# Two slabs of a state-space projection formed by seven block products, with the stage's parameters loaded a stage earlier

## The reference, cut to what matters

```
zxbcdt = x @ w_in                      # (256,1024) @ (1024,6208)
z, xbc, dt = split(zxbcdt, [2048, 6144])
xbc = silu(conv5(xbc, conv_w) + conv_b)    # depthwise over the tokens
xs, bm, cm = split(xbc, [2048, 3072])
dt = softplus(dt + dt_bias)
y = scan forwards (xs, dt_f, -exp(a_log[0]), bm, cm) + scan backwards + xs * d_skip
y = rms_norm_by_group(y * silu(z)) * norm_w
return y @ w_out
```

## Time and profile before

| | us |
|---|---|
| median of 3 runs | 2305.78 |
| lowest and highest | 2304.95 and 2306.76 |
| the profiled execution: its time | 2306.97 |
| its span, first to last instruction | 2305.1 |

### The profile page before, as it was taken

One profiled execution on the slowest core, in us unless ns is written; L12 is line 12 of the kernel. 1 busy time (PEld: TensorE's weight loads), 2 busy tenths in 40 slices (PEclk: granted clock), 3 DMA queues, 4 the chain that ended last, 5 costly groups with the idle time before them and its releaser, 6 DMA issues.

```text
span 2305.1 us, 25572 instructions
## 1 busy us (share of the span) xinstructions
PE 2269.1 (98%) x10790; PEld 1371.1 (59%) x10790; DVE 979.0 (42%) x1950; ACT 443.7 (19%) x1011; POOL 73.8 (3%) x130
## 2 busy tenths in 40 slices
PE   9999999999999999999999999999999999999998
PEld 6568547886487459997434433335999643333342
DVE  3567646667576557653211111125774311111122
ACT  3410003258110011220211211101132121111111
POOL 2000000000000000000000000000000000000000
PEclk9999999999999999999999999999999999999999
DMA  7279625354698415246999999995426599999997
GB/s 292 113 306 401 257 78 204 147 183 173 243 407 327 178 59 203 97 176 262 382 429 427 427 427 428 427 418 193 164 96 247 223 409 427 427 429 427 427 428 285
DMA packets 59168, 671.64 MB, mean 291 GB/s; under 512 B 7505, under 2 KB 7793, under 8 KB 18721
## 3 DMA queue, kind: packets, MB, share of 16 engines
q1 hardware_dynamic: 51888, 649.45, 69.1%
q0 software_dynamic: 7152, 20.43, 2.6%
HBM read 666.59 MB, written 3.26 MB: 291 GB/s over the span
## 4 chain that ended last, share of the span: by engine, by line
PE 87%; DMA 10%; DVE 3%; issue 0%; ACT 0%; SPq 0%; POOL 0%; DVEq 0%; POOLq 0%; ACTq 0%
PE ps L101 84%; DMA ring<-in_exp_w 8%; DVE arena L114 1%; PE ps L349 1%; DVE arena L117 1%; DMA arena<-ssm_rows 1%; PE ps L2753 1%; DMA ring<-in_ada_w 0%; PE ps L638 0%; DMA ring<-in_attn_w_in 0%; PE ps L1915 0%; DVE X L117 0%; PE ps L1234 0%; ACT arena L106 0%; DVE arena L110 0%
## 5 line engine op out<-in xcount | busy, mean ns | idle before, releaser
L101 PE MATMUL ps<-arena 128*64 128x512 f32 (+8 forms) x4036 | 954.6, 465 | 16.2 <-DMA arena<-in_exp_w 5.9
L101 PEld LDWEIGHTS ps<-arena 128*128 128x128 f32 (+2 forms) x4036 | 462.4, 167 | 464.5 <-issue 434.6
L101 PE MATMUL ps<-ring,arena 128*64 128x512 f32 (+2 forms) x1720 | 460.7, 584 | 3.2 <-DMA ring<-in_exp_w 3.2
L101 PE MATMUL ps<-XTGB,ring 128*128 128x256 f32 (+1 forms) x2160 | 423.5, 353 | 0.0
L101 PEld LDWEIGHTS ps<-XTGB,ring 128*128 128x128 f32 x2160 | 367.4, 191 | 52.5 <-issue 11.2
L101 PEld LDWEIGHTS ps<-ring,arena 128*64 128x64 f32 (+1 forms) x1720 | 174.9, 151 | 259.5 <-issue 253.9
L122 DVE COPY arena<-ps 128x512 f32<-128x512 f32 (+5 forms) x133 | 63.3, 496 | 417.4 <-PE ps L101 298.6
L121 ACT COPY arena<-ps 128x512 f32<-128x512 f32 (+3 forms) x179 | 81.5, 474 | 676.2 <-PE ps L2753 283.7
L101 PE MATMUL ps<-XTGB,arena 128*64 128x512 f32 (+2 forms) x736 | 200.7, 428 | 0.0
L105 ACT ACTIVATE arena<-ps 128x512 f32<-128x512 f32 (+2 forms) x95 | 51.2, 545 | 679.4 <-PE ps L101 674.6
L101 PE MATMUL ps<-ring,XTGB 128*128 128x512 f32 (+3 forms) x484 | 168.5, 503 | 2.9 <-DMA ring<-in_attn_w_in 2.7
(11 more groups left out here) (151 smaller groups left out, 949.8 us busy)
## 6 DMA issues: line engine op xcount, KB each, us to landing
arena<-in_exp_w SPq DMA_DIRECT2D x90, 2048.0 KB, 26.7
ring<-in_exp_w SPq DMA_DIRECT2D x68, 2048.0 KB, 27.9
ring<-in_mlp_w SPq DMA_DIRECT2D x25, 2048.0 KB, 8.8
ring<-in_ada_w SPq DMA_DIRECT2D x20, 2048.0 KB, 9.6
XTGB<-in_exp_w SPq DMA_DIRECT2D x18, 2048.0 KB, 32.3
ring<-in_ssm_w_in SPq DMA_DIRECT2D x12, 2048.0 KB, 7.6
ring<-in_w_in SPq DMA_DIRECT2D x12, 2048.0 KB, 7.8
ring<-in_gate_w SPq DMA_DIRECT2D x12, 2048.0 KB, 7.5
```

Source lines behind the costliest of these rows:

```text
L101: return self.e.matmul(o, lhsT=lhsT, rhs=rhs, start=start, stop=stop, skip_group_check=True)
```

## The change

Slabs 5 and 6 are formed by seven products of blocks in place of eight. The slab is cut into halves of its input channels and of its columns, `XT` into halves of its input channels and of the tokens; with the blocks X1, X2 (channels) and W the four blocks, the products are of single blocks (1 and 2), or of sums of blocks (3 to 7). VectorE forms the sums: four of `XT`'s blocks once (`sw_x_sums`), four of the weights' blocks for each slab (`sw_sums`, three of them, one in place in the slab, and `sw_last_sum`). The sums for slab 5 and three of those for slab 6 stand at the end of `mlp0_dve`, ahead of the row pass; slab 6's last one stands behind the first convolution. A product is 2 column blocks x 4 chunks = 8 matmuls with 128 moving columns; the seven go into four banks a slab (`SW_GROUPS`). ScalarE copies product 1 straight into an input buffer of the convolution, VectorE adds the others there (`sw_results`), and the copy of the whole bank falls away for these slabs. There are four input buffers in place of two, so eight memsets of the edges in place of four, and VectorE waits for them at its start as well. The four parameter loads move from `ssm_pool` to `mlp0_pool`.

```diff
--- before.py
+++ after.py
@@ -1106,6 +1106,10 @@
             pool.stage("mlp0")
             pool.wait_ge(at("XT", 1, 1))
             ada_b_pool(pool, 0, ab0)
+            pool.landed(pool.e.dma_start(prm, d["ssm_conv"].rearrange("p (a b) -> p a b", a=32)), "ssmp", "ssmp")
+            pool.landed(pool.e.dma_start(dd, d["ssm_dn"]), "ssmp", "ssmp")
+            pool.landed(pool.e.dma_start(dtb, bcast(d["ssm_dt_bias"][0:1, :])), "ssmp", "ssmp")
+            pool.landed(pool.e.dma_start(ang, bcast(d["ssm_A_log"][0:1, :])), "ssmp", "ssmp")
             keep_mod(pool, 0)
             for t in range(2):
                 rstd(pool, lrs[:, t:t + 1], at("var", 2, t), ("rstd", 2, t))
@@ -1128,6 +1132,10 @@
             for t in range(2):
                 blocks_out(v, 0, 2, t, sU0)
                 norm_turned(v, 2, t)
+            sw_x_sums(v)
+            sw_sums(v, 5)
+            sw_last_sum(v, 5)
+            sw_sums(v, 6)
             norm_rows_all(v, 2, at("gb", "ln2"))
 
 
@@ -1145,7 +1153,7 @@
         dtt = arena.get(2, 64)
         aa = arena.get(2, 64)
         s_pos = arena.pos
-        s_u = [arena.get(2, 260) for _ in range(2)]
+        s_u = [arena.get(2, 260) for _ in range(4)]
         s_v = [arena.get(2, T) for _ in range(2)]
         s_tok = arena.get(2, 512)
         CONV = [2, 3, 0, 1] + list(range(4, 16))
@@ -1163,6 +1171,93 @@
         tri = C["tri"]
         LE, GE, LEO, OGE = tri[:, 0:P], tri[:, 384:512], tri[:, 0:T], tri[:, T:512]
         drow = nc.dram_tensor("ssm_rows", (16, 1024), F32).ap()
+        room = arena.pos
+        arena.pos = zT.shape[1] * T + xcT.shape[1] * T
+        swX = [arena.get(4, P) for _ in range(4)]
+        swS = [[arena.get(4, T) for _ in range(2)] for _ in range(2)]
+        swS4 = arena.get(4, T)
+        arena.pos = room
+        SW_GROUPS = ((1, 6), (5, 7), (3, 4), (2,))
+        def conv_in(n):
+            return s_u[n % 2 + (2 if n in (4, 5) else 0)]
+        def sw_x_sums(v):
+            x1, x2, x3, x4 = swX
+            v.wait_ge(at("XT", 2, 0), at("XT", 2, 1))
+            k = v.then_inc(v.tt(x1, XT[:, 0:4, P:T], XT[:, 0:4, 0:P], ALU.subtract), "swX")
+            v.then_inc(v.tt(x3, XT[:, 4:8, P:T], XT[:, 0:4, P:T], ALU.subtract), "swX")
+            v.wait_ge(k)
+            k = v.then_inc(v.tt(x2, XT[:, 4:8, P:T], x1, ALU.subtract), "swX")
+            v.wait_ge(k)
+            v.then_inc(v.tt(x4, XT[:, 4:8, 0:P], x2, ALU.subtract), "swX")
+        def sw_sums(v, s):
+            w = weights(("sw", s))
+            s1, s2 = swS[s % 2]
+            v.wait_ge(at("w", ("sw", s)))
+            k = v.then_inc(v.tt(s1, w[:, 0:4, T:2 * T], w[:, 4:8, T:2 * T], ALU.add), ("swS", s, 5))
+            v.wait_ge(k)
+            k = v.then_inc(v.tt(s2, s1, w[:, 0:4, 0:T], ALU.subtract), ("swS", s, 6))
+            v.then_inc(v.tt(w[:, 0:4, T:2 * T], w[:, 0:4, 0:T], w[:, 0:4, T:2 * T], ALU.subtract), ("swS", s, 7))
+        def sw_last_sum(v, s):
+            s1, s2 = swS[s % 2]
+            v.wait_ge(at("swS", s, 6), at("swp", s - 1, 2) if s == 6 else None)
+            v.then_inc(v.tt(swS4, weights(("sw", s))[:, 4:8, 0:T], s2, ALU.subtract), ("swS", s, 3))
+        def sw_products(pe, s):
+            w = weights(("sw", s))
+            s1, s2 = swS[s % 2]
+            x1, x2, x3, x4 = swX
+            pairs = {1: (XT[:, 0:4, 0:P], w[:, 0:4, 0:T]), 2: (XT[:, 4:8, 0:P], w[:, 4:8, 0:T]), 3: (XT[:, 4:8, P:T], swS4),
+                     4: (x4, w[:, 4:8, T:2 * T]), 5: (x1, s1), 6: (x2, s2), 7: (x3, w[:, 0:4, T:2 * T])}
+            pe.wait_ge(at("w", ("sw", s)), at("swX"))
+            for r, group in enumerate(SW_GROUPS):
+                ps = bank(pe, "swp", s, r)
+                for n, p in enumerate(group):
+                    x, y = pairs[p]
+                    if p in (3, 5, 6, 7):
+                        pe.wait_ge(at("swS", s, p))
+                    for f in range(2):
+                        for c in range(4):
+                            ins = pe.mm(ps[:, n * T + f * P:n * T + (f + 1) * P], y[:, c, f * P:(f + 1) * P], x[:, c, :],
+                                        c == 0, c == 3)
+                pe.then_inc(ins, ("swp", s, r), *([("free", ("sw", s))] if r == 3 else []))
+        def sw_product(s, r, n):
+            return ps_of("swp", s, r)[:, n * T:(n + 1) * T].rearrange("p (f t) -> p f t", f=2)
+        def sw_parts(s):
+            n = 0 if s == 5 else 4
+            return [conv_in(n + k)[:, :, o:o + P] for k in range(2) for o in (2, 2 + P)]
+        def sw_results(v, s, r):
+            c11, c12, c21, c22 = sw_parts(s)
+            def plus(o, q, n, x, *done):
+                return v.then_inc(v.tt(o, sw_product(s, q, n), x, ALU.add), ("read", "swp", s, q), *done)
+            v.wait_ge(at("swp", s, r))
+            if r == 0:
+                v.wait_ge(at("swP1", s))
+                plus(c12, 0, 1, c11, ("swU2", s))
+            elif r == 1:
+                v.wait_ge(at("swU2", s))
+                e = plus(c21, 1, 1, c12)
+                plus(c12, 1, 0, c12, ("swU4", s))
+                v.wait_ge(e)
+                plus(c22, 1, 0, c21, ("conv in", s, 1), ("swU3", s))
+            elif r == 2:
+                v.wait_ge(at("swU3", s), at("swU4", s))
+                plus(c12, 2, 0, c12, ("conv in", s, 0))
+                plus(c21, 2, 1, c21, ("conv in", s, 1))
+            else:
+                plus(c11, 3, 0, c11, ("conv in", s, 0))
         SP = 16
 
         def ssm_sp(sp):
@@ -1176,10 +1271,6 @@
         def ssm_pool(pool):
             pool.stage("ssm")
             pool.wait_ge(at("XT", 2, 1))
-            pool.landed(pool.e.dma_start(prm, d["ssm_conv"].rearrange("p (a b) -> p a b", a=32)), "ssmp", "ssmp")
-            pool.landed(pool.e.dma_start(dd, d["ssm_dn"]), "ssmp", "ssmp")
-            pool.landed(pool.e.dma_start(dtb, bcast(d["ssm_dt_bias"][0:1, :])), "ssmp", "ssmp")
-            pool.landed(pool.e.dma_start(ang, bcast(d["ssm_A_log"][0:1, :])), "ssmp", "ssmp")
             for u in s_u:
                 pool.then_inc(pool.e.memset(u[:, :, 0:2], 0.0), "u0")
             for u in s_u:
@@ -1258,7 +1349,10 @@
                     turn_rows(pe, 2, 1, X, at("x", 2, 1))
                 gemm_t1(pe, ("sdt",), "sdt", 64, t)
             for s in range(5, 12):
-                gemm_f(pe, ("sw", s), ("sw", s), 4)
+                if s < 7:
+                    sw_products(pe, s)
+                else:
+                    gemm_f(pe, ("sw", s), ("sw", s), 4)
                 if s == 5:
                     for fp in range(2):
                         ps = bank(pe, "sw", 4, fp)
@@ -1333,6 +1427,12 @@
                 act.wait_ge(at("st", t))
                 act.then_inc(act.cp(s_tok[:, t, :], ps_of("st", t)), "s tok", ("read", "st", t))
 
+            def first_product(s):
+                act.wait_ge(at("swp", s, 0))
+                act.then_inc(act.cp(sw_parts(s)[0], sw_product(s, 0, 0)), ("swP1", s), ("read", "swp", s, 0))
+            first_product(5)
             def conv_out(n):
                 i = CONV[n]
                 act.wait_ge(at("conv", i))
@@ -1340,12 +1440,17 @@
 
             for n, i in enumerate(CONV):
                 s, fp, f0 = 4 + i // 2, i % 2, 2 * i
-                u, v_ = s_u[n % 2], s_v[n % 2]
-                act.wait_ge(at("sw", s, fp))
+                u, v_ = conv_in(n), s_v[n % 2]
+                if n == 3:
+                    first_product(6)
                 if n >= 2:
                     act.wait_ge(at("conv", CONV[n - 2]))
-                k = act.then_inc(act.cp(u[:, :, 2:258], two(ps_of("sw", s, fp))), ("read", "sw", s, fp))
-                act.wait_ge(k)
+                if s in (5, 6):
+                    act.wait_ge(at("conv in", s, fp), at("xc", CONV[n - 2]) if n >= 2 else None)
+                else:
+                    act.wait_ge(at("sw", s, fp))
+                    k = act.then_inc(act.cp(u[:, :, 2:258], two(ps_of("sw", s, fp))), ("read", "sw", s, fp))
+                    act.wait_ge(k)
                 for q in range(2):
                     act.then_inc(act.act(v_[:, q, :], u[:, q, 0:T], ACT.Identity, scale=prm[:, f0 + q, 0:1],
                                          bias=prm[:, f0 + q, 5:6]), ("conv0", i, q))
@@ -1412,10 +1517,10 @@
 
         def ssm_dve(v):
             v.stage("ssm")
-            v.wait_ge(at("XT", 2, 1), at("ssmp"))
+            v.wait_ge(at("XT", 2, 1), at("ssmp"), at("u0"))
 
             def conv(n, i):
-                u, v_ = s_u[n % 2], s_v[n % 2]
+                u, v_ = conv_in(n), s_v[n % 2]
                 for q in range(2):
                     f = 2 * i + q
                     v.wait_ge(at("conv0", i, q))
@@ -1440,8 +1545,17 @@
             k = v.then_inc(v.ts(aa, dtt, -1.0, None, ALU.mult))
             v.wait_ge(k)
             v.then_inc(v.tt(aa, aa, dtt, ALU.min), "dt min")
+            for r in range(4):
+                sw_results(v, 5, r)
             for n, i in enumerate(CONV):
                 conv(n, i)
+                if n == 0:
```

(6 more changed lines are left out.)

## The result

The changed kernel takes 2311.89 us (median of 8 runs, 2308.77 to 2315.44), the kernel before 2305.57 (8 runs beside them): ratio 1.0029, 95% interval 1.0019 to 1.0039. It is slower by 6.3 us, outside the range of 2302.5 to 2308.5; the forecast was no change.

What follows compares the result with a forecast made beforehand. TensorE, busy 98% of the span, was taken as the bound; slab 5's +0.66 us, including a 2.0 us stall, and slab 6's saving of 1.33 summed to -0.7 us: 2305.1 us forecast, range 2302.5 to 2308.5.

Steps and rivals of the forecast that it cites:

- The products: TensorE, slabs 5 and 6: 112 records of 0.1115 us make 12.49 us a slab, saving 1.33 each, 2.66 together.
- (2): Slabs 5 and 6: products show no gain at 0.127 us a record; +1.8 us, 2307.6; chance 0.14 together with (4).
- (3): Slabs 5 and 6: weight loads do not hide behind 128 columns; +15 us, 2321; chance 0.04.
- the estimate of 324 ns a matmul: TensorE's block products: four passes of about 81 ns per f32 matmul, 18.1 us a slab, some 8.7 us lost.
- The sums, the row pass, the memsets, the bank: Stage start: VectorE's sums delay row pass, memsets and ScalarE's copy, so TensorE stalls 2.0 us at slab 5's third bank.
- (1): Slab 5: no wait at the third bank; -2.66 us, 2303.1; chance 0.16.
- the sum: Whole change: slab 5 takes 0.66 us more, slab 6 saves 1.33, together -0.7 us.
- (4): Slab 6's last sum misses its 1.6 us margin; with 2 us beyond, +1.3, 2307.1; chance 0.14 together with (2).
- The cover of the moved loads: Parameter loads left in place would land some 11 us after first issue, TensorE standing still that long; the move covers this.
- moves with TensorE alone: Behind slab 6: VectorE, some 6 us later, catches up by slab 10, so only TensorE's change shifts the scan's start.
- what was not seen: Anywhere in the program: effects outside the named cases, chance 0.04, half to each side.

Runs made afterwards that it cites:

- early edges: Changed kernel with the eight edge memsets moved from the state-space stage to right behind the moved parameter loads: 2308.97 us, ratio 1.0016.
- padded changed kernel: Changed kernel with 16 matmuls added to the first expert stage's general path, which is jumped over and never runs: 2307.65 us, ratio 1.0011.
- the padding: 16 matmuls added to the never-run path; on the changed kernel with the edge memsets also moved early: 2303.33 us, ratio 0.9992.
- 44 matmuls: Kernel before with 44 matmuls added to the general path that is jumped over and never runs: 2305.09 us in a single execution.

## Why the prediction was wrong

**The products.** Right: 32 records from 362.73 to 366.30 are 0.1116 us each, 0.1115 was taken; without the wait two slabs save 45.58 - 42.96 = 2.62 us, 2.66 was the sum. Rivals (2) and (3) are out. With them goes, for these f32 products, the estimate of 324 ns a matmul that the prediction made by the pairing rule of the Trainium skill's "TensorE: Matmul & The Clock Gate" ("Back-to-back issue gap"): the trace has 223.

**The sums, the row pass, the memsets, the bank.** Right in each link: the row pass ends 362.91 + 4.87 = 367.8 us, ScalarE starts at 369.7 (370.4 and 372.2 in the prediction, both less the 2.9 us of the span's start: 367.5 and 369.3), and TensorE waits 2.12 us, where 2.0 was said. Rival (1) is out in the changed kernel; the early edges show that it takes only the memsets' place to make it true. The stage gains 0.25 us in the profiled execution, 0.7 was the sum: TensorE resumes at 370.37, 0.3 us later than said (372.95 less 2.89). VectorE adds seven results a slab, not the eight that the prediction counted (12 sums and 14 additions are the 26 instructions that it has more); no wait of TensorE depended on it. No wait shows inside slab 6 or behind slab 8, so rival (4) is out. The cover of the moved loads was sized too high: with the loads in their old place the last one landed 6.3 us behind the first one's issue (369.27 to 375.59), not 11, and TensorE stood still for 8.0 us.

**What the wait costs.** Mis-sized in one of the two executions profiled that have it. In the padded changed kernel the same wait of 2.13 us is followed by a product at half pace, 3.48 us instead of 1.89:

```profile
368.54 1.95 PE L101 MATMUL ps<-arena,ring 128*128 128x128 f32 x16
372.62 3.64 PE L101 MATMUL ps<-XTGB,arena 128*128 128x128 f32 x16 [2.13 <-ACT arena L121]
376.10 1.95 PE L101 MATMUL ps<-arena,ring 128*128 128x128 f32 x16
```

The busy times in short windows tell why: the granted clock (the column in front of the DMA share) fell to 0.51, the lower of the two levels, and came back. The first row is the changed kernel's, with its wait and the product behind it at a granted clock of 1.00; the other three are the padded one's.

```profile
368.00:372.00 4.00, 1.88 (x17) 1.69 (x16) 1.59 (x6) 1.35 (x3) 1.50 (x11) 1.00 0.94 395
372.00:374.00 2.00, 1.38 (x6) 1.38 (x7) 1.34 (x6) 1.33 (x3) 0.00 (x0) 0.64 0.80 330
374.00:376.00 2.00, 2.00 (x12) 2.00 (x11) 1.05 (x3) 0.00 (x0) 0.00 (x0) 0.51 0.88 348
376.00:378.00 2.00, 2.00 (x20) 2.00 (x20) 0.00 (x0) 0.00 (x0) 0.00 (x0) 1.00 0.10 39
```

There the stage loses 1.36 us. So it is worth -0.24 or +1.36 us, by the clock; the early edges gain 4.3 us of the median with the padding, and 3.0 without it by the ratios (1.0029 and 1.0016), more than the 2.1 of the wait.

**The step that failed** is the last one, which carries the stage's change to the end of the program: "A change of -0.7 gives 2306.3 and 2305.1". That the scan's start "moves with TensorE alone" held, but any change further on was put at nothing, without a reason, with only a chance of 0.04 for what was not seen. The 48 added matmuls were costed by their columns and their weight loads, and not as code: they push all of TensorE's later instructions on by 193 places, and some 1180 us later the block behind a jump ends in the wrong spot. That is +5.2 us by the trace, shown by moving the code alone: away in the changed kernel, there in the kernel before (12.70 - 8.19 = 4.5 us), small at 44 matmuls. With -0.24 to +1.36 from the stage it makes +5.0 to +6.6 us, beside 6.3 measured. The case was in no row that I read: the 4.13 us of TensorE's wait for "issue" at this jump stood in the trace of before, and I did not look outside the stage.

The Trainium skill, "Runtime: NRT & Kernel Launch", section "Instruction fetch mechanics", says that instructions come in blocks of 16 KB fetched ahead in sequence, and that a taken branch to a place not yet held must first fetch its block. The trace agrees as far as it goes (packets of 1.47 MB / 90 = 16 KB, and 1.43 and 1.45 us of waiting behind the rows' being ready in the two kernels).

What stays open: which of the changed kernel's runs lost the clock, and why the padded changed kernel's median is still 1.7 us above the kernel before. The padded kernel's trace was granted half the clock near 1111 and near 1415 us as well, where the trace of the kernel before has 1.00, and is 1.5 us longer between slab 8 and the jump. Of its eleven runs the three slowest (2310.71 to 2313.83) have the lowest mean granted clock, 0.993. That fits a lost clock; that the change brings it about is not shown.

## What to carry to other kernels

Instructions have a place as well as a duration: if a program holds a jump, look in the trace at what the engine does right behind it, and after any change that adds or removes instructions ahead of it, look again before you credit or blame the edit. A few never-run instructions in the skipped path move the code without changing what runs; here that tested it cleanly and took the stall away. And a wait on the bounding engine is priced with the clock that it may lose, which in one execution here came to 1.6 us for a wait of 2.1.

## What the runs showed of the hardware

Behind the jump the work of the second block of instructions began 5.8 to 6.0 us after the first record of the first one, in all four kernels profiled that ran into its end (1566.34 - 1560.42 = 5.9 in the changed one). The same wait of TensorE, 2.12 and 2.13 us, left the granted clock at 1.00 in one execution and at 0.51 in another.
